# Uneven token sets, later second sums and a denser last step in the layer boundary of a diffusion backbone

## The reference

```
ada = silu(cond) @ w_ada[i] + b_ada[i]
shift, scale, gate = split(ada, 3)
h = rmsnorm(x, norm_pre[i]) * (1 + scale) + shift
m = mixer(h)                        # ends in  gated @ w_out
x = x + gate * rmsnorm(m, norm_post[i])
```

## Time and profile before

| | us |
|---|---|
| median of 3 runs (4850.35 to 4858.61) | 4855.77 |
| the profiled execution's own time | 4852.59 |
| span of its trace | 4850.8 |
| TensorE busy in the span | 4264.6 (88%) |
| VectorE busy | 2707.8 (56%) |
| ScalarE busy | 2088.7 (43%) |
| matmuls of line 2316, 2304 of them | 417.7 busy |
| mean granted clock of TensorE, as a share of full | 0.96 |

### The profile page before, as it was taken

How to read it: one execution, slowest core, us unless ns; L and a number is a source line. 1 busy time by engine, 2 the same in 40 slices (tenths; PEclk the granted TensorE clock), 3 DMA queues, 4 the chain that set the end, 5 groups by cost and what they waited for, 6 DMA issues and landing times. The chain is left out here.

```text
span 4850.8 us, 136580 instructions
## 1 busy us (share of the span) xinstructions
PE 4264.6 (88%) x60744; PEld 3645.3 (75%) x60744; DVE 2707.8 (56%) x4582; ACT 2088.7 (43%) x3758; POOL 2.7 (0%) x8
## 2 busy tenths in 40 slices
PE   3699997999998889988889899998999789999968
PEld 0388876888886778956667799986887678888848
DVE  0552346777775653255556633367424477777745
ACT  0543223555554554156664400056432245555553
POOL 0000000000000000000000000000000000000000
PEclk7899998999999999989999999999999899999989
DMA  9134485333333310100001011112445733333241
GB/s 417 68 103 128 142 249 164 90 89 95 95 95 131 109 60 32 52 24 1 1 1 36 14 44 39 43 61 81 119 122 174 237 120 95 91 89 90 81 177 61
DMA packets 535832, 475.30 MB, mean 98 GB/s; under 512 B 27616, under 2 KB 499040, under 8 KB 530784
## 3 DMA queue, kind: packets, MB, share of 16 engines
q1 hardware_dynamic: 404448, 400.73, 25.4%
q10 hardware_dynamic: 130816, 66.07, 5.0%
HBM read 338.00 MB, written 128.71 MB: 96 GB/s over the span
## 5 line engine op out<-in xcount | busy, mean ns | idle before, releaser
L593 PE MATMUL ps<-big_r,stage_r 128*128 128x384 f32 x2976 | 640.9, 350 | 16.1 <-DVE big_r L824 14.8
L593 PEld LDWEIGHTS ps<-big_r,stage_r 128*128 128x128 f32 x2976 | 522.2, 189 | 100.2 <-issue 55.1
L2316 PE MATMUL ps<-big_r,w_out 128*128 128x384 f32 x2304 | 417.7, 341 | 38.0 <-DVE w_out L2432 37.9
L2316 PEld LDWEIGHTS ps<-big_r,w_out 128*128 128x128 f32 x2304 | 407.8, 191 | 46.2 <-DVE w_out L2432 41.0
L593 PE MATMUL ps<-big_r,w_slab_r 128*128 128x384 f32 x1488 | 341.1, 337 | 0.0
L380 PE MATMUL ps<-big_r,stage_r 128*128 128x384 f32 x1536 | 309.3, 335 | 14.7 <-DVE big_r L367 14.7
L2103 DVE TENSOR_REDUCE extra<-ps 128x1 f32<-128x1152 f32 (+1 forms) x144 | 171.8, 1234 | 224.2 <-PE ps L2015 224.2
L380 PEld LDWEIGHTS ps<-big_r,stage_r 128*128 128x128 f32 x1536 | 270.8, 188 | 16.9 <-issue 14.6
L1367 ACT COPY arena<-ps 128x512 f32<-128x512 f32 x288 | 168.9, 587 | 254.7 <-PE ps L1172 254.2
L593 PEld LDWEIGHTS ps<-big_r,w_slab_r 128*128 128x128 f32 x1488 | 268.7, 189 | 0.0
L1521 DVE COPY_PREDICATED arena<-arena,ps 128x128 f32<-128x128 uint32 x720 | 193.1, 325 | 120.7 <-PE ps L1160 120.2
(11 more groups left out here) (250 smaller groups left out, 8314.5 us busy)
## 6 DMA issues: line engine op xcount, KB each, us to landing
w_slab<-in_w SPq DMA_DIRECT2D x138, 512.0 KB, 3.5
scan_in<-x_resid ACTq DMA_DIRECT2D x112, 576.0 KB, 5.5
arena<-in_w_ada SPq DMA_DIRECT2D x24, 2048.0 KB, 27.5
arena<-scan_in SPq DMA_DIRECT2D x144, 320.0 KB, 3.8
arena<-scan_in SPq DMA_DIRECT2D x288, 128.0 KB, 3.8
arena<-scan_in SPq DMA_DIRECT2D x48, 576.0 KB, 7.8
arena<-scan_in SPq DMA_DIRECT2D x144, 192.0 KB, 3.9
scan_y<-arena SPq DMA_DIRECT2D x144, 128.0 KB, 2.1
```

The source lines that it names most:

```text
L593: mm = pe.matmul(g.ps[:, 3 * s + c, 0:CW], w[:, k * P:(k + 1) * P], x[:, k, chunk(c)], start=k == i == 0, stop=k == NB - 1 and i == 2)
L2316: mm = pe.matmul(g.ps[:, bank(i, b), 0:wide[i]], w[:, b, k * P:(k + 1) * P], r, start=k == j == 0, stop=k == NB - 1 and j == 2)
```

## The change

The sets become 512, 384 and 256 tokens instead of three times 384. In the last step three tables of their own put two blocks of `residual` behind each of units 1 to 4, with squares and results to match. `sum2`, `mean2` and `root2` of set i - 1 come behind unit 7 of step i and no longer behind unit 6. The buffers of `square2` move from the arena into the two weight slab buffers (the 512-token set takes more of the arena for its high halves), and for that the loads of the next mixer's first two slabs wait until the last of the squares has been summed (`last_mm`), and stand in SP's queue behind the writes of `x` and the wait for them.

```diff
-CHUNKS = ((0, 384), (384, 768), (768, 1152))
+CHUNKS = ((0, 512), (512, 896), (896, 1152))
 ROWS_AT = ((0, 1, 2), (3,), (), (), (4, 5), (6,), (7,), ())
 RESIDUAL_AT = ((), (0,), (1, 2, 3), (4, 5, 6), (7,), (), (), ())
 SQUARE_AT = ((), (), (0, 1, 2), (3, 4, 5), (6,), (7,), (), ())
 RESULT_AT = ((), (), (0,), (1, 2, 3), (4,), (5,), (6,), (7,))
+RESIDUAL_LAST = ((), (0, 1), (2, 3), (4, 5), (6, 7), (), (), ())
+SQUARE_LAST = ((), (0,), (1, 2), (3, 4), (5, 6), (7,), (), ())
+RESULT_LAST = ((), (0,), (1, 2), (3,), (4,), (5,), (6,), (7,))
...
-    assert at + 6 * 512 <= 4 * n
+    assert at + 4 * 512 <= 4 * n
...
-    sq2 = [g.arena[:, at + 2048 + 512 * i:at + 2560 + 512 * i] for i in range(2)]
+    sq2 = [g.slab[:, i, 0:512] for i in range(2)]
...
                 sp.dma_start(g.slab[:, b % WSLOTS, :], g.io["w"][base + b]).then_inc(slab_in[b % WSLOTS], 16)
-            if follows:
-                sp.wait_ge(wl_ok, NB)
-                for s in range(WSLOTS):
-                    sp.dma_start(g.slab[:, s, :], g.io["w"][mixer_slabs(layer + 1) + s]).then_inc(next_in, 16)
-                sp.wait_ge(next_in, 16 * WSLOTS)
             dest = g.io["y"] if last else g.x_kept[1] if MIXER[layer + 1] != 2 else None
             if dest is not None:
                 for i in range(LAST + 1):
                     sp.wait_ge(x_ok, NB * (i + 1))
                     sp.dma_start(dest[:, :, tokens(i)], g.x[:, :, tokens(i)]).then_inc(x_st, 16)
                 sp.wait_ge(x_st, 16 * (LAST + 1))
+            if follows:
+                sp.wait_ge(last_mm, NB)
+                for s in range(WSLOTS):
+                    sp.dma_start(g.slab[:, s, :], g.io["w"][mixer_slabs(layer + 1) + s]).then_inc(next_in, 16)
+                sp.wait_ge(next_in, 16 * WSLOTS)
...
-                    if i and b == 6 and not last:
+                    if i and b == 7 and not last:
                         sum2(i - 1)
...
             def square2(i, b):
                 act.wait_ge(x_ok, NB * i + b + 1)
+                if i == b == 0:
+                    act.wait_ge(wl_ok, NB)
...
-                    for k in RESULT_AT[b]:
+                    for k in (RESULT_LAST if i == LAST else RESULT_AT)[b]:
                         result(i, k)
                     if b == 0:
                         root1(i - 1)
                     if last:
                         continue
-                    for k in SQUARE_AT[b]:
+                    for k in (SQUARE_LAST if i == LAST else SQUARE_AT)[b]:
                         square2(i - 1, k)
-                    if b == 6:
+                    if b == 7:
                         root2(i - 1)
...
-                        for k in RESIDUAL_AT[b]:
+                        for k in (RESIDUAL_LAST if i == LAST else RESIDUAL_AT)[b]:
                             residual(i - 1, k)
                             if k and not last:
                                 add2(i - 1, k - 1)
                         if b == 5 and not last:
                             add2(i - 1, NB - 1)
-                        if b == 6 and not last:
+                        if b == 7 and not last:
                             mean2(i - 1)
```

## The result

The change made the kernel slower. In 7 runs each the median went from 4853.03 to 4869.97 us; the ratio is 1.0031, with a 95% interval from 1.0021 to 1.0041 (the ratios here are the recorded ones with their intervals; they can differ a little from the quotient of the medians, which is 1.0035). The forecast was +16.1 us and 4871.9. The profiled execution has a span of 4868.2 us, 17.4 more than before.

The account below looks back on a forecast made before the run. TensorE bounds most of the boundaries, but in the shorter step 2 DVE's late chain on set 1 would. Three boundaries 6.6 us longer and the last 3.7 shorter give +16.1 us, 4871.9 against the median; range 4862 to 4881.

Parts of the forecast that it names:

- Widths and start: Matmuls of 226.5 ns at 512 columns on a straight line; all four boundaries' step 0 ends 10.6 us later.
- The rival that a 512-column matmul costs no more than the 173 ns of a 384-column one: All boundaries: seven units of step 0 cost 9 us less than forecast per boundary, kernel at 4836; chance 2%.
- Step 1: TensorE stays at 4.155 us a unit, the `sum2` stall goes, DVE's chain grows 1.5 us, last unit at 34.1.
- the old stall: TensorE's wait for DVE at `sum2` in step 1, 0.57 us; its removal was to gain 0.8 to 1.3 us.
- Step 2: DVE's chain on set 1 from 52.2 to 67.2, after TensorE's last unit at 59.8; `residual(2)` 9.6 us later.
- rivals with free turns: Turns cost nothing and the tail is shorter: each boundary loses 4.5 us, +9.8 in all; chance 14%.
- with TensorE as the bound of this step: Step 2 stays bound by TensorE, last unit ready at 58.6, kernel faster at 4840.7; chance 5%.
- Tail and loads: From `residual(2)` to the end 16.4 to 16.6 us for 19.4, 3.0 saved; slab loads land at 15.9.
- just hidden: End of boundaries 1 and 3: late slab loads land 15.9 us into the tail, at worst 17.6; ACT ends at 16.4.
- the rival with the loads exposed: SP's last landing ends boundaries 1 and 3, 1.2 us later each, kernel at 4874.3; chance 15%.
- The last boundary: After the last layer, no second sums: shorter units and residuals and a sooner last write, sum -3.7 us.

Follow-up runs that it names:

- the run at unit 6: Changed kernel with `sum2`, `mean2` and `root2` back behind unit 6 in both steps: boundaries 146.4, 146.4, 149.7 and 118.4 us, against 141.2, 141.2, 144.6 and 118.3.
- the old tables run: Changed kernel with the old tables of residual, squares and results in the last step too: boundaries 140.1, 140.1, 143.6 and 118.4 us.
- The four runs with the root first: `root first` on the changed kernel: alone, with equal sets, with old tables, and with old tables and two `shifted` later; first boundary 137.4, 135.3, 135.4 and 134.0 us.
- the run with `shifted` spread: Changed kernel with the eight `shifted(0)` spread over step 2 behind the root of set 1: boundaries 141.3, 141.3, 144.9 and 118.3 us.
- root first: Changed kernel with `shifted(0)` spread over step 2 and `scaled(0)` behind the mean of set 1: boundaries 137.4, 137.4, 141.0 and 118.4 us.

## Why the prediction was right

**Widths and start.** Right in every term: 227 ns at 512 columns and 120 at 256, rows 1.07 us apart, step 0 longer by 10.4 for 10.6. The rival that a 512-column matmul costs no more than the 173 ns of a 384-column one is out.

**Step 1.** Right: no stall at `sum2(0)`, last unit at 34.2. The sum for DVE's chain on set 0 was wrong, though. It took off the shorter splits of all eight rows, but only three of them, rows 4, 5 and 6, stand inside the chain: +2.5 us and not +1.5. Before, that chain ended at 30.25, so the 32.6 that I stated is not what my sum gives (31.8), and that the trace has 32.7 is luck. It cost nothing, as the last unit still came later. What I did not see is how much the move of the second sums was worth. I put its gain at the old stall, 0.8 to 1.3 us; with these sets the run at unit 6 shows 5.2, because the work behind the wait in DVE's queue stands behind a unit that comes late and, at the lower clock, takes longer.

**Step 2.** The step that decides, and right: chain from 52.3 for 52.2, 14.8 us long for 15.0, with the turns of the new tables in it (1.1 us by the old tables run), a bank wait of 1.03 for 1.1, TensorE done 7.2 us before `sum2(1)`. Two terms are not quite what their parts give: 47.4, 4.15 and 0.9 make 52.4 and not 52.2, and from 52.9 to 53.7 it is 0.8 and not 1.1 (the bank came free at 53.9). The rivals with free turns and with TensorE as the bound of this step are out. From the chain's end to `scaled(1)` it took 4.7 us for the 4.3 that I had read off the tail; the sum itself ran at the lower clock (a granted 0.50 from 1742.57 to 1744.22), 1.65 us for 0.81, and that is most of it: in the run with 448, 384 and 320 tokens a sum of 0.91 us goes with 4.2 us, one of 1.65 with 4.7.

**The cause, tested.** The four runs with the root first show that the late start of the chain is the cost, and only in a short step 2: the edit wins 3.8 us there and nothing with equal sets. They also correct me on one point. I had named ACT only as what delays the start. Once the start is early, ACT's total work in step 2 is the next bound: the run with `shifted` spread starts the chain 3 us earlier and wins nothing, 3.3 us or more off my expectation, and root first was 1.4 us off or more.

**Tail and loads.** 16.3 us for 16.4. The loads land 16.2 us into the tail for 15.9, 0.1 us ahead of ACT's end, so "just hidden" was right by very little, and the rival with the loads exposed is out; starting them earlier changed nothing. Its worst case adds up to 17.3 us and not 17.6, so the rival was priced 0.3 us a boundary too high.

**The last boundary.** -3.8 for -3.7, the write included.

**Size.** The four boundaries and the last write give +15.4 us for the +16.1 forecast; the medians differ by 16.9. The 0.7 is made of four small terms that all have the same sign, of which the second boundary is the largest (+6.2 for +6.6). I had taken the tail of the first boundary, 19.4 us, for all three, and in the second it was 19.8 before the change: the granted clock over the 8 us from 79 on was 0.86 in the first boundary and 0.67 in the second. That the medians come within 0.8 us of the forecast is partly luck, as the stretches that the change does not touch differ by more.

## What to carry to other kernels

In a pipeline of a few unequal stages like this one, a shorter last stage pays only if the work that runs beside it, one stage late, still ends before it does: compare the two ends, not the busy shares. When a chain is late, look first at what stands ahead of its first instruction in the queues; here a finished set's scaling stood before the root on which eight blocks waited. And a queue order that spreads such work must leave the end of the stage free for what the next sum needs.

## What the runs showed of the hardware that I had not expected

A wait of 2.8 us in the midst of dense matmuls cost more than its length. In the run with the second sums at unit 6 the granted clock was 1.00 before it and 0.77 over the 6 us behind the sum, and the two units behind it, one of 384 columns and one of 256, took 8.97 us where 4.155 and 2.87 and the last matmul's end make 7.3. (The timeline merges both units into one line and shows the first one's width.) After waits of 7 to 8 us a sum of 384 columns took 1.65 us for 0.81, and a unit of 256 columns 5.26 for 3.0. The length of the wait alone does not decide it: after 3.43 us the same sum took 0.91 us in the first boundary of one run, at a granted clock of 1.00, and 1.65 us in its third, at 0.50. The 0.57 us wait of the kernel before had no such effect: the sum after it took 0.91 us, and the granted clock over the 30 us from 1690 on was 1.00.
